# Two of the four weight sums in each block of seven products made by adding transfers instead of VectorE, in a two-layer encoder on one core

## The chip, the cores and the metric

The kernel runs on one core of one Trainium2 chip. The metric is the device time of one execution, in microseconds (us). TensorE (PE in the rows) multiplies, VectorE (DVE) and ScalarE (ACT) prepare its operands and take its results, GpSimd (POOL) and SyncE (SP) issue transfers; PEld is TensorE's weight load, which runs beside its matmuls. Each engine executes its own instructions in the order in which they are written and waits on semaphores.

## The reference, cut to what matters

Two layers, each with a mixer (differential attention, then gated linear attention) and a dense MLP, on 256 rows of 2048 values, all in float32. The change lies in the second matrix product of the two MLPs alone:

```python
def squared_relu_mlp(x, w1, w2):          # x (256, 2048), w1 (2048, 8192), w2 (8192, 2048)
    return jnp.square(jax.nn.relu(x @ w1)) @ w2
...
    for i in range(DEPTH):                # DEPTH = 2
        ...
        f = squared_relu_mlp(h, mlp_w1[i], mlp_w2[i])
        h = layer_norm(DN_ALPHA * h + f, ln_g[i, 1], ln_b[i, 1])
```

## The kernel before

**Splitting.** Every weight tile is 128 partitions x 4 rows x 512 columns of float32, 1 MB. A transfer issued by SP brings it into one of four slots `raw[:, j]`. ScalarE rounds it into `hi` (`split_hi`, `quarter_hi`), VectorE forms `lo = raw - hi` (`split_lo`, `quarter_lo`), and TensorE multiplies by `hi` and `lo` of the tile and of the activations. `hi` and `lo` also have four slots, so each tile goes through raw, hi, lo and TensorE in a pipeline. The counters are `raw_full[j]` (tile landed), `hi_ready`, `lo_ready`, `w_used` (TensorE is done with a tile). SP waits on `lo_ready` before it loads into a slot again.

**A chunk of the MLP.** `mlp(m)` has 4 chunks of 2048 hidden values. In each, four groups of four tiles (`up_pair`) make the hidden values. Then the second product follows, in two halves of the output's columns (`fast_pair`, q = 0 and q = 2; in the last chunk q = 2 is done by plain groups). So there are 7 such blocks in each MLP and 14 in the program. A block, called a unit here, consists of:

- seven products of one tile each, `product(g, p, ...)` with p = 0 to 6, a fast scheme for a 2 x 2 block product. They take quarters of the weight matrix and sums of quarters: the stationary operand is a part of the activations (`F`) or a sum of such parts (`forms`). Each product has 8 matmuls by `hi` and then 4 by `lo`;
- four plain tiles, "the rest" (r0 to r3 below), L763 to L771, 24 matmuls each.

**The quarters.** `load_quarters` brings W00, W01, W11, W10 into slots 0, 1, 2, 3. VectorE makes four sums in place with `w_sum` (L1454): slot 0 += slot 1 (for product 1), slot 1 += slot 2 (for product 4), slot 0 += slot 2 (for product 2), slot 3 += slot 0 (for product 6). Products 0, 3 and 5 take W00, W10 and W11 as loaded. Between these, VectorE adds the products' results to `res` with `add_part` (L1465); TensorE may start a product that accumulates in a bank only when `res_added` tells that the bank was read.

**Names in the text.** T0 is the start of a unit's product 0 on TensorE. "lo p" is VectorE's `quarter_lo` for product p, "hi p" ScalarE's `quarter_hi`. `first_adds` and `second_adds` add the results of the previous unit's rest tiles. `load_rest` loads r0 to r3. POOL has nothing to do while the MLPs' units run, except for a load of the layer norm's vectors at the end of each MLP.

Of the kernel before, what the change touches and what calls it, by code (L numbers as in the profile page):

```python
# [26 lines left out]
F32 = mybir.dt.float32  # L27
# [60 lines left out]
SUMMED = [0, 8 * CHUNKS - 4]  # L88
# [4 lines left out]
def build(nc, x, attn_w_qkv, attn_w_o, attn_lambda, attn_subln, gla_w_in, gla_w_gk2, gla_b_gk,  # L93
          gla_norm, gla_w_o, mlp_w1, mlp_w2, ln_g, ln_b, out):
    ctx = ExitStack()
    with ctx:
# [125 lines left out]
        w_summed = sem("w_summed")  # L222
        set_up = sem("set_up")
# [72 lines left out]
        def _(sp):  # L296
# [7 lines left out]
            def load_quarters(g, w, row, q):  # L304

                for j, (k, n) in enumerate(((0, 0), (0, 1), (1, 1), (1, 0))):
                    sp.wait_ge(lo_ready, 4 * g + j - 3)
# [30 lines left out]
            def load_mlp(m):  # L338
                for ch in range(CHUNKS):
                    with sp.Fori(0, QUARTERS) as q:  # L340
                        load_group(STEP * ch + q + G_MLP[m], w_1[m], D * ch + COLS * q)
                    load_quarters(STEP * ch + (G_MLP[m] + 4), w_2[m], KT * ch, 0)
                    load_rest(STEP * ch + (G_MLP[m] + 6), w_2[m], KT * ch, 0)
                    if ch < CHUNKS - 1:
                        load_quarters(STEP * ch + (G_MLP[m] + 7), w_2[m], KT * ch, 2)
                        load_rest(STEP * ch + (G_MLP[m] + 9), w_2[m], KT * ch, 2)
# [22 lines left out]
        def _(pool):  # L369
            def load_gb(layer, i):  # L370
                for n, src in enumerate((ln_g, ln_b)):
                    pool.dma_start(ln_gb[:, n, :], src[layer, i].partition_broadcast(P)).then_inc(gb_loaded, 16)

# [47 lines left out]
            scale_residual(1)  # L421
            pool.wait_ge(w_used, 4 * (G_MLP[0] + STEP * (CHUNKS - 1) + 6))
# [47 lines left out]
            scale_residual(3)  # L470
            pool.wait_ge(w_used, 4 * (G_MLP[1] + STEP * (CHUNKS - 1) + 6))
# [417 lines left out]
        def _(act):  # L889
            def split_hi(g, j, f=None):  # L890

                act.wait_ge(raw_full[j], 16 * (g if f is None else f) + 16)
                if not isinstance(g, int) or g:
                    act.wait_ge(w_used, 4 * g + j - 3)
                act.activation(hi[:, j], raw[:, j], ACT.Copy).then_inc(hi_ready, 1)  # L895
# [5 lines left out]
            def split_all(g, f=None):  # L901
                split_some(g, TILES, f)
# [137 lines left out]
            def quarter_hi(g, p, j, f, w):  # L1040

                if p in (0, 3, 5):
                    act.wait_ge(raw_full[j], 16 * f + 16)
                else:
                    act.wait_ge(w_summed, w + {1: 1, 2: 3, 4: 2, 6: 4}[p])
# [25 lines left out]
            def chunk(m, ch, g, f, n, first, last):  # L1071

                k = 8 * ch + 32 * m
                u = 4 * ch + FORMED[m]
                w = 8 * ch + SUMMED[m]
# [11 lines left out]
                for p, j in ((0, 0), (1, 0), (2, 0), (3, 3), (4, 1), (5, 2), (6, 3)):  # L1087
                    quarter_hi(g + 4, p, j, f + 4, w)
                down_halves(g + 3, n + 3, 1, k + 6, u + 4, False)
                split_some(g + 6, 2, f + 5)  # L1090
                f_hi_of(1, k + 6, 12)
                split_hi(g + 6, 2, f + 5)
                split_hi(g + 6, 3, f + 5)
                if last:
                    split_all(g + 7, f + 6)
                    split_all(g + 8, f + 7)
                else:
                    for p, j in ((0, 0), (1, 0), (2, 0), (3, 3), (4, 1), (5, 2), (6, 3)):
# [108 lines left out]
        def _(dve):  # L1207
            def split_lo(g, j):

                dve.wait_ge(hi_ready, 4 * g + j + 1)  # L1210
                dve.tensor_tensor(lo[:, j], raw[:, j], hi[:, j].bitcast(F32), ALU.subtract).then_inc(lo_ready, 1)  # L1211
# [290 lines left out]

            def fast_adds(s, reads, b, q):

                add_part(0, q, b, 4 * s + 1)
                quarter_lo(s, 3, 3)
                w_sum(3, 0)
                add_part(0, q + 1, b, 4 * s + 3, ALU.subtract)
                quarter_lo(s, 4, 1)
                add_part(1, q + 1, b + 1, 4 * s + 2)  # L1510
                quarter_lo(s, 5, 2)
                dve.wait_ge(res_added, reads + 3)
                add_part(1, q + 1, b, 4 * s + 5, ALU.subtract)
                quarter_lo(s, 6, 3)
# [13 lines left out]
            def chunk(m, ch, g, f, n, r, w, first, last):  # L1528
# [253 lines left out]
```

## Time and profile before

| | |
|---|---|
| median of 3 runs | 2183.89 us (2183.36 to 2185.74) |
| profiled execution, its own time | 2181.14 us |
| its span | 2179.4 us |
| PE / PEld busy | 2160.6 / 1845.6 us |
| DVE / ACT / POOL busy | 1544.2 / 995.5 / 110.3 us |
| granted TensorE clock, mean | 0.998 |
| moved by DMA | 417.20 MB, mean 191 GB/s |

The difference between an execution's time and its span is 1.7 us here and lies outside the kernel's instructions. Busy times are unions of an engine's instructions. A matmul's end is modelled and overlaps the next one, so a short wait of TensorE may not show as idle time on PE; it shows as idle time before a weight load on PEld, and as a late start.

### The profile page before, as it was taken

The numbers are of one execution on the slowest core, as the hardware profiler recorded it, in microseconds if no ns is written. First come the engines' busy times: TensorE is split into PE (matmuls) and PEld (weight loads), VectorE is DVE, ScalarE is ACT, GpSimd is POOL, SyncE is SP. The second block draws the span as 40 slices with busy tenths as digits, with TensorE's granted clock in tenths as the row PEclk, the third lists the DMA queues.
The fourth block names the chain that finished last, engine by engine and source line by source line (L and its number), as shares of the span: only waits on it lengthen the run. The fifth ranks groups of instructions, "written<-read, shape, count | busy, mean of one in ns | idle before, by whom it ended". The sixth has DMA issues, their size and how long they took to land.

```text
span 2179.4 us, 27756 instructions
## 1 busy us (share of the span) xinstructions
PE 2160.6 (99%) x11162; PEld 1845.6 (85%) x11162; DVE 1544.2 (71%) x1292; ACT 995.5 (46%) x831; POOL 110.3 (5%) x95
## 2 busy tenths in 40 slices
PE   9999999999999999999999999999999999999997
PEld 8888888988888888888888888889878888888886
DVE  5554555879678678767776566658796796786686
ACT  5443543445445444444454344334454454454541
POOL 3000000200000000000020111102000000000000
PEclk9999999999999999999999999999999999999999
DMA  9545546545754854764546445646367448547552
GB/s 318 169 156 176 181 178 220 176 134 186 264 167 154 272 190 154 250 191 183 204 140 230 160 155 185 234 158 208 103 236 245 135 168 275 173 154 270 188 209 105
DMA packets 206653, 417.20 MB, mean 191 GB/s; under 512 B 6688, under 2 KB 6688, under 8 KB 205552
## 3 DMA queue, kind: packets, MB, share of 16 engines
q1 hardware_dynamic: 204672, 406.09, 54.7%
q0 software_dynamic: 1472, 9.25, 1.2%
q8 instruction: 55, 0.90, 0.2%
q10 hardware_dynamic: 432, 0.79, 0.1%
q14 instruction: 22, 0.18, 0.0%
HBM read 414.00 MB, written 2.10 MB: 191 GB/s over the span
## 4 chain that ended last, share of the span: by engine, by line
PE 84%; DVE 7%; DMA 4%; issue 2%; ACT 2%; POOLq 0%; POOL 0%; DVEq 0%; ACTq 0%; SPq 0%
PE ps L479 71%; PE ps L719 5%; DMA raw<-in_mlp_w_dram 4%; DVE lo L1450 2%; PE ps L763 2%; PE ps L765 2%; PE ps L771 2%; DVE raw L1454 2%; ACT hi L895 1%; DVE lo L1211 1%; ACT hi L1047 1%; PE ps L550 1%; DVE res L1465 1%; DMA res<-in_x_dram 0%; PE ps L648 0%
## 5 line engine op out<-in xcount | busy, mean ns | idle before, releaser
L1211 DVE TENSOR_TENSOR lo<-raw,hi 128x2048 fp32r<-128x2048 f32 x328 | 751.2, 2304 | 328.6 <-ACT hi L895 326.7
L895 ACT ACTIVATE hi<-raw 128x2048 fp32r<-128x2048 f32 x327 | 624.1, 1916 | 584.9 <-PE ps L479 412.6
L479 PE MATMUL ps<-X,hi 128*128 128x512 f32 (+1 forms) x3008 | 700.1, 378 | 1.5 <-DVE X L1223 0.9
L479 PEld LDWEIGHTS ps<-X,hi 128*128 128x128 f32 x3008 | 542.7, 189 | 95.6 <-DVE X L1223 1.1
L479 PE MATMUL ps<-X,lo 128*128 128x256 f32 x2816 | 386.9, 283 | 0.0
L479 PEld LDWEIGHTS ps<-X,lo 128*128 128x128 f32 x2816 | 373.2, 191 | 12.8
L1047 ACT ACTIVATE hi<-raw 128x2048 fp32r<-128x2048 f32 x98 | 186.3, 1917 | 199.9 <-DVE raw L1454 142.9
L1450 DVE TENSOR_TENSOR lo<-raw,hi 128x2048 fp32r<-128x2048 f32 x98 | 224.1, 2287 | 33.0 <-ACT hi L1047 33.0
L479 PE MATMUL ps<-hi,X 128*128 128x512 f32 x768 | 246.7, 396 | 0.0
L479 PE MATMUL ps<-hi,F 128*128 128x512 f32 x768 | 241.0, 391 | 0.1
L763 PE MATMUL ps<-hi,F 128*128 128x512 f32 x448 | 175.0, 391 | 2.5 <-ACT hi L895 2.4
L765 PE MATMUL ps<-hi,F 128*128 128x512 f32 x448 | 174.4, 389 | 0.0
L479 PEld LDWEIGHTS ps<-hi,F 128*128 128x128 f32 x768 | 144.2, 188 | 30.8 <-DVE lo L1211 0.9
L479 PEld LDWEIGHTS ps<-hi,X 128*128 128x128 f32 x768 | 144.2, 188 | 30.6 <-issue 1.0
L479 PE MATMUL ps<-lo,X 128*128 128x512 f32 x384 | 149.6, 389 | 0.0
L479 PE MATMUL ps<-lo,F 128*128 128x512 f32 x384 | 149.5, 389 | 0.0
L1454 DVE TENSOR_TENSOR raw<-raw 128x2048 f32<-128x2048 f32 x56 | 126.8, 2285 | 0.0
L719 PE MATMUL ps<-hi,forms 128*128 128x512 f32 x448 | 111.2, 390 | 1.4 <-DVE res L1465 1.4
L771 PE MATMUL ps<-lo,F 128*128 128x512 f32 x448 | 110.6, 389 | 0.0
L763 PEld LDWEIGHTS ps<-hi,F 128*128 128x128 f32 x448 | 84.1, 188 | 22.4 <-ACT hi L895 5.1
L1465 DVE TENSOR_TENSOR res<-res,ps 128x512 f32<-128x512 f32 x112 | 74.1, 682 | 38.3 <-PE ps L719 19.2
L719 PEld LDWEIGHTS ps<-hi,forms 128*128 128x128 f32 x448 | 83.8, 188 | 20.3 <-issue 1.8
(141 smaller groups left out, 1533.1 us busy)
## 6 DMA issues: line engine op xcount, KB each, us to landing
raw<-in_mlp_w_dram SPq DMA_DIRECT2D x256, 1024.0 KB, 5.9
raw<-in_gla_w_in_dram SPq DMA_DIRECT2D x48, 1024.0 KB, 5.3
raw<-in_attn_w_qkv_dram SPq DMA_DIRECT2D x47, 1024.0 KB, 5.2
raw<-in_attn_w_o_dram SPq DMA_DIRECT2D x16, 1024.0 KB, 5.9
raw<-in_gla_w_o_dram SPq DMA_DIRECT2D x16, 1024.0 KB, 6.5
work<-in_ln_g_dram POOLq DMA_DIRECT2D x4, 1024.0 KB, 7.9
work<-in_ln_b_dram POOLq DMA_DIRECT2D x4, 1024.0 KB, 10.3
out_dram<-res SPq DMA_DIRECT2D x8, 256.0 KB, 2.5
```

The lines of the kernel that those rows point to most:

```text
L479: return pe.matmul(o, w, m, start=start, stop=stop)
L550: m = pe.transpose(ps[:, LN_BANKS[i % 3], blk(b)], res[:, t, blk(4 * q + b)], ident[:, :])
L719: return pe.matmul(o, w, m, start=first, stop=last or not start, skip_group_check=not start)
L763: pe.matmul(acc, F[:, a, 0, blk(t)], hi[:, p, k, :], start=first, stop=True, skip_group_check=not first)
L765: pe.matmul(acc, F[:, a, 1, blk(t)], hi[:, p, k, :], start=False, stop=True, skip_group_check=True)
L771: e = pe.matmul(acc, F[:, 4 * j + k, 0, blk(t)], lo[:, p, k, :], start=False, stop=True, skip_group_check=True)
L895: act.activation(hi[:, j], raw[:, j], ACT.Copy).then_inc(hi_ready, 1)
L1047: act.activation(hi[:, p % TILES], raw[:, j], ACT.Copy).then_inc(hi_ready, 2 if p == PRODUCTS - 1 else 1)
L1211: dve.tensor_tensor(lo[:, j], raw[:, j], hi[:, j].bitcast(F32), ALU.subtract).then_inc(lo_ready, 1)
L1450: dve.tensor_tensor(lo[:, p % TILES], raw[:, j], hi[:, p % TILES].bitcast(F32), ALU.subtract).then_inc(lo_ready, 2 if p == PRODUCTS - 1 el ...
L1454: dve.tensor_tensor(raw[:, j], raw[:, j], raw[:, k], ALU.add).then_inc(w_summed, 1)
L1465: dve.tensor_tensor(d, d, ps[:, bank, :], op).then_inc(res_added, 1)
```

## The change

Two of the four sums leave VectorE. `weight_sums` on POOL issues a transfer from DRAM with `accum_op=ADD`, which adds a weight quarter to what is in the slot: W11 onto slot b (W01) once VectorE has used W01 in its first sum, and W10 onto slot a (W00+W01+W11) once lo 2 is done. The other two sums stay on VectorE. Product 4 now waits for `third_added` and product 6 for `fourth_added`. The number of SP's loads is the same; POOL issues 28 more transfers of 1 MB.

Slots have roles a, b, c, d instead of fixed numbers. Slot d (W10) is no longer summed into, so it is free after lo 3, b after lo 4, c after lo 5 and a, the last, after lo 6. `load_rest` fills them in that order (d, b, c, a), where it before filled slot 0 and 1 after lo 4. The next unit's roles turn accordingly (`SLOTS`, `TURNED`). In the last chunk the roles are set so that the plain groups behind find slots 0 to 3 in order.

On VectorE lo 2 moves behind the first `add_part`, and `first_adds` no longer stands between sums. On ScalarE the hi of r0 moves ahead of `down_halves`.

```diff
+SLOTS = (0, 1, 2, 3)
+TURNED = (3, 1, 2, 0)
...
-            def load_rest(g, w, row, q):
-
-                for j, (n, k) in enumerate(((0, 2), (1, 2), (0, 3), (1, 3))):
-                    sp.wait_ge(lo_ready, 4 * g - (3, 3, 2, 0)[j])
+            def load_rest(g, w, row, q, slots):
+
+                for i, (j, (n, k)) in enumerate(zip(slots, ((0, 2), (1, 2), (0, 3), (1, 3)))):
+                    sp.wait_ge(lo_ready, 4 * g - (4, 3, 2, 0)[i])
...
+            def weight_sums(m):
+
+                for u in range(UNITS[1]):
+                    ch, q = u // 2, u % 2 * 2
+                    a, b = (SLOTS if ch < CHUNKS - 1 and q == 0 else TURNED)[:2]
+                    below = w_2[m][:, KT * ch + KPT:KT * ch + 2 * KPT, :]
+                    pool.wait_ge(w_summed, 2 * (UNITS[m] + u) + 1)
+                    pool.dma_start(raw[:, b], below[:, :, (q + 1) * COLS:(q + 2) * COLS], accum_op=ALU.add
+                                   ).then_inc(third_added, 16)
+                    pool.wait_ge(lo_ready, 4 * (G_MLP[m] + STEP * ch + (4 if q == 0 else 7)) + 3)
+                    pool.dma_start(raw[:, a], below[:, :, q * COLS:(q + 1) * COLS], accum_op=ALU.add
+                                   ).then_inc(fourth_added, 16)
...
+            def quarters_hi(g, f, u, slots):
+
+                a, b, c, d = slots
+                quarter_hi(g, 0, a, raw_full[a], 16 * f + 16)
+                quarter_hi(g, 1, a, w_summed, 2 * u + 1)
+                quarter_hi(g, 2, a, w_summed, 2 * u + 2)
+                quarter_hi(g, 3, d, raw_full[d], 16 * f + 16)
+                quarter_hi(g, 4, b, third_added, 16 * u + 16)
+                quarter_hi(g, 5, c, raw_full[c], 16 * f + 16)
+                quarter_hi(g, 6, a, fourth_added, 16 * u + 16)
...
-            def quarter_sums(s, f, between=None):
-
-                quarter_lo(s, 0, 0)
-                dve.wait_ge(raw_full[1], 16 * f + 16)
-                w_sum(0, 1)
-                dve.wait_ge(raw_full[2], 16 * f + 16)
-                w_sum(1, 2)
-                quarter_lo(s, 1, 0)
-                w_sum(0, 2)
-                if between:
-                    between()
-                quarter_lo(s, 2, 0)
-
-            def fast_adds(s, reads, b, q):
-
+            def quarter_sums(s, f, slots):
+
+                a, b, c, _ = slots
+                quarter_lo(s, 0, a)
+                dve.wait_ge(raw_full[b], 16 * f + 16)
+                w_sum(a, b)
+                quarter_lo(s, 1, a)
+                dve.wait_ge(raw_full[c], 16 * f + 16)
+                w_sum(a, c)
+
+            def fast_adds(s, reads, b, q, slots):
+
+                w, x, y, z = slots
                 add_part(0, q, b, 4 * s + 1)
-                quarter_lo(s, 3, 3)
-                w_sum(3, 0)
+                quarter_lo(s, 2, w)
+                quarter_lo(s, 3, z)
                 add_part(0, q + 1, b, 4 * s + 3, ALU.subtract)
-                quarter_lo(s, 4, 1)
                 add_part(1, q + 1, b + 1, 4 * s + 2)
-                quarter_lo(s, 5, 2)
+                quarter_lo(s, 4, x)
+                quarter_lo(s, 5, y)
                 dve.wait_ge(res_added, reads + 3)
                 add_part(1, q + 1, b, 4 * s + 5, ALU.subtract)
-                quarter_lo(s, 6, 3)
+                quarter_lo(s, 6, w)
...
                 if not last:
-                    quarter_sums(g + 7, f + 6, lambda: first_adds(g + 4, 2 * r, 0, 0))
-                    fast_adds(g + 7, 2 * r + 6, 4, 2)
+                    quarter_sums(g + 7, f + 6, TURNED)
+                    first_adds(g + 4, 2 * r, 0, 0)
+                    fast_adds(g + 7, 2 * r + 6, 4, 2, TURNED)
```

VectorE in the unit q = 2 of a chunk, before: lo 0 (L1450), two sums (L1454), lo 1, a sum, the two `first_adds` (L1465), lo 2, then `add_part`, lo 3 and the fourth sum, and so on to lo 6.

```order
L1450 TENSOR_TENSOR lo<-raw,hi 128x2048
L1454 TENSOR_TENSOR raw<-raw 128x2048 x2
L1450 TENSOR_TENSOR lo<-raw,hi 128x2048
L1454 TENSOR_TENSOR raw<-raw 128x2048
L1465 TENSOR_TENSOR res<-res,ps 128x512 x2
L1450 TENSOR_TENSOR lo<-raw,hi 128x2048
L1465 TENSOR_TENSOR res<-res,ps 128x512
L1450 TENSOR_TENSOR lo<-raw,hi 128x2048
L1454 TENSOR_TENSOR raw<-raw 128x2048
L1465 TENSOR_TENSOR res<-res,ps 128x512
L1450 TENSOR_TENSOR lo<-raw,hi 128x2048
```

The same stretch of the changed kernel (L1481 is `quarter_lo`, L1485 `w_sum`, L1496 `add_part`), from lo 0 to lo 6:

```order
L1481 TENSOR_TENSOR lo<-raw,hi 128x2048
L1485 TENSOR_TENSOR raw<-raw 128x2048
L1481 TENSOR_TENSOR lo<-raw,hi 128x2048
L1485 TENSOR_TENSOR raw<-raw 128x2048
L1496 TENSOR_TENSOR res<-res,ps 128x512 x3
L1481 TENSOR_TENSOR lo<-raw,hi 128x2048 x2
L1496 TENSOR_TENSOR res<-res,ps 128x512 x2
L1481 TENSOR_TENSOR lo<-raw,hi 128x2048 x2
L1496 TENSOR_TENSOR res<-res,ps 128x512
L1481 TENSOR_TENSOR lo<-raw,hi 128x2048
```

Two sums are gone, the two `first_adds` and the unit's first `add_part` now stand in one row before lo 2, and lo 2 and lo 3 follow one another.

ScalarE of the changed kernel at the end of the first unit's products in a chunk, with the semaphores (L1066 is `quarter_hi`, the last L916 are the rest tiles, L1092 `down_halves`):

```order
L1066 ACTIVATE hi<-raw 128x2048 [waits w_used,raw_full0]
L1066 ACTIVATE hi<-raw 128x2048 [waits w_used,w_summed] x2
L1066 ACTIVATE hi<-raw 128x2048 [waits w_used,raw_full3]
L1066 ACTIVATE hi<-raw 128x2048 [waits w_used,third_added]
L1066 ACTIVATE hi<-raw 128x2048 [waits w_used,raw_full2]
L1066 ACTIVATE hi<-raw 128x2048 [waits w_used,fourth_added]
L916 ACTIVATE hi<-raw 128x2048 [waits w_used,raw_full3]
L1092 ACTIVATE work<-ps 128x512 [waits form_summed,f_lo,w_used]
L1092 ACTIVATE work<-ps 128x512
L916 ACTIVATE hi<-raw 128x2048 [waits w_used,raw_full1]
```

hi 4 and hi 6 waited for VectorE's `w_summed` before; now they wait for the two adding transfers, and the hi of r0, `down_halves` and all later tiles stand behind hi 6.

## Rows read from the trace of the kernel before

**Rows 1.** The page, part 1: busy us, share, instructions.

```profile
PE 2160.6 (99%) x11162; PEld 1845.6 (85%) x11162; DVE 1544.2 (71%) x1292; ACT 995.5 (46%) x831; POOL 110.3 (5%) x95
```

**Rows 2.** Groups by line and shape: busy us, mean ns | idle before, releasers.

```profile
L1450 DVE TENSOR_TENSOR lo<-raw,hi 128x2048 fp32r<-128x2048 f32 x98 | 224.1, 2287 | 33.0 <-ACT hi L1047 33.0
L1047 ACT ACTIVATE hi<-raw 128x2048 fp32r<-128x2048 f32 x98 | 186.3, 1917 | 199.9 <-DVE raw L1454 142.9 <-PE ps L479 26.8 <-PE ps L719 19.5
L479 PEld LDWEIGHTS ps<-hi,F 128*128 128x128 f32 x768 | 144.2, 188 | 30.8 <-DVE lo L1211 0.9
L1454 DVE TENSOR_TENSOR raw<-raw 128x2048 f32<-128x2048 f32 x56 | 126.8, 2285 | 0.0
L763 PEld LDWEIGHTS ps<-hi,F 128*128 128x128 f32 x448 | 84.1, 188 | 22.4 <-ACT hi L895 5.1
L719 PEld LDWEIGHTS ps<-hi,forms 128*128 128x128 f32 x448 | 83.8, 188 | 20.3 <-issue 1.8 <-DVE res L1465 1.2
L1465 DVE TENSOR_TENSOR res<-res,ps 128x512 f32<-128x512 f32 x112 | 74.1, 682 | 38.3 <-PE ps L719 19.2 <-PE ps L771 19.1
L719 PEld LDWEIGHTS ps<-lo,F 128*128 128x128 f32 x168 | 31.3, 188 | 6.9 <-DVE lo L1450 0.5
```

**Rows 3.** PEld in order of time: start, us, what [idle before <- releaser].

```profile
703.69 1.68 PEld L719 LDWEIGHTS ps<-hi,forms 128*128 128x128 f32 x8 [0.87 <-issue]
...
1629.38 0.19 PEld L763 LDWEIGHTS ps<-hi,F 128*128 128x128 f32 x1 [1.97 <-ACT hi L895]
```

**Rows 4.** PE in order of time, a unit q = 2 of the first MLP.

```profile
700.37 1.98 PE L719 MATMUL ps<-hi,forms 128*128 128x512 f32 x8
702.18 1.07 PE L719 MATMUL ps<-lo,forms 128*128 128x512 f32 x4
703.70 2.10 PE L719 MATMUL ps<-hi,forms 128*128 128x512 f32 x8 [0.45 <-DVE res L1465]
```

**Rows 5.** The chain that ended last: start, us, what.

```profile
567.94 89.04 PE ps L479 x512
...
710.80 5.08 DMA raw<-in_mlp_w_dram
...
740.02 89.04 PE ps L479 x512
...
911.05 89.04 PE ps L479 x512
...
1621.03 6.36 DMA raw<-in_mlp_w_dram
```

**Rows 6.** DVE in order of time, the same unit q = 2.

```profile
687.51 2.29 DVE L1450 TENSOR_TENSOR lo<-raw,hi 128x2048 fp32r<-128x2048 f32 x1 [0.86 <-ACT hi L1047]
...
700.68 2.29 DVE L1450 TENSOR_TENSOR lo<-raw,hi 128x2048 fp32r<-128x2048 f32 x1 [0.87 <-ACT hi L1047]
702.89 0.68 DVE L1465 TENSOR_TENSOR res<-res,ps 128x512 f32<-128x512 f32 x1
703.48 2.29 DVE L1450 TENSOR_TENSOR lo<-raw,hi 128x2048 fp32r<-128x2048 f32 x1
```

**Rows 7.** A lone 1 MB load issued by POOL: its issue row, and us to landing.

```profile
318.69 0.61 POOL L372 DMA_DIRECT2D work<-in_ln_g_dram  x1 [4.85 <-PE ps L648]
...
work<-in_ln_g_dram POOLq DMA_DIRECT2D x1, 1024.0 KB, 4.7
```

**Rows 8.** The transfers in 1015 to 1045: GB/s in 40 slices, and issues.

```profile
GB/s 404 404 388 388 396 380 388 385 393 388 390 456 418 396 404 391 415 423 418 355 407 380 388 390 382 385 393 388 382 388 385 388 300 363 407 390 229 287 399 369
...
work<-in_ln_g_dram POOLq DMA_DIRECT2D x1, 1024.0 KB, 9.1
work<-in_ln_b_dram POOLq DMA_DIRECT2D x1, 1024.0 KB, 11.7
```

**Rows 9.** Busy us by stage: PE, PEld, DVE, ACT, POOL, PEclk, DMA share, GB/s.

```profile
672.00:698.00 26.00, 26.00 (x116) 21.52 (x115) 24.69 (x16) 12.65 (x8) 0.00 (x0) 1.00 0.80 291
698.00:740.00 42.00, 41.24 (x181) 33.43 (x180) 35.45 (x24) 22.69 (x12) 0.00 (x0) 1.00 0.65 228
```

More of the change, by code:

```diff
@@ L87 @@
 FORMED = [0, 4 * CHUNKS]
-SUMMED = [0, 8 * CHUNKS - 4]
+SLOTS = (0, 1, 2, 3)
+TURNED = (3, 1, 2, 0)
 UNITS = [0, 2 * CHUNKS - 1]
@@ L222, in build @@
         w_summed = sem("w_summed")
+        third_added = sem("third_added")
+        fourth_added = sem("fourth_added")
         set_up = sem("set_up")
@@ L302, in load_group, with load_quarters @@
                                  ).then_inc(raw_full[j], 16)
-            def load_quarters(g, w, row, q):
-                for j, (k, n) in enumerate(((0, 0), (0, 1), (1, 1), (1, 0))):
-                    sp.wait_ge(lo_ready, 4 * g + j - 3)
+            def load_quarters(g, w, row, q, slots, quarters=((0, 0), (0, 1), (1, 1), (1, 0))):
+                for i, (j, (k, n)) in enumerate(zip(slots, quarters)):
+                    sp.wait_ge(lo_ready, 4 * g + i - 3)
                     sp.dma_start(raw[:, j], w[:, bass.ds(row + KPT * k, KPT), (q + n) * COLS:(q + n + 1) * COLS]
                                  ).then_inc(raw_full[j], 16)
-            def load_rest(g, w, row, q):
-                for j, (n, k) in enumerate(((0, 2), (1, 2), (0, 3), (1, 3))):
-                    sp.wait_ge(lo_ready, 4 * g - (3, 3, 2, 0)[j])
+            def load_rest(g, w, row, q, slots):
+                for i, (j, (n, k)) in enumerate(zip(slots, ((0, 2), (1, 2), (0, 3), (1, 3)))):
+                    sp.wait_ge(lo_ready, 4 * g - (4, 3, 2, 0)[i])
                     sp.dma_start(raw[:, j], w[:, bass.ds(row + KPT * k, KPT), (q + n) * COLS:(q + n + 1) * COLS]
@@ L421, in _ @@
             scale_residual(1)
+            weight_sums(0)
             pool.wait_ge(w_used, 4 * (G_MLP[0] + STEP * (CHUNKS - 1) + 6))
@@ L470, in _ @@
             scale_residual(3)
+            weight_sums(1)
             pool.wait_ge(w_used, 4 * (G_MLP[1] + STEP * (CHUNKS - 1) + 6))
@@ L889, in _, with split_hi @@
         def _(act):
-            def split_hi(g, j, f=None):
-                act.wait_ge(raw_full[j], 16 * (g if f is None else f) + 16)
+            def split_hi(g, j, f=None, slots=SLOTS):
+                act.wait_ge(raw_full[slots[j]], 16 * (g if f is None else f) + 16)
                 if not isinstance(g, int) or g:
                     act.wait_ge(w_used, 4 * g + j - 3)
-                act.activation(hi[:, j], raw[:, j], ACT.Copy).then_inc(hi_ready, 1)
+                act.activation(hi[:, j], raw[:, slots[j]], ACT.Copy).then_inc(hi_ready, 1)
             def split_some(g, n, f=None):
@@ L899, in split_some, with split_all @@
                     split_hi(g, j, f)
-            def split_all(g, f=None):
-                split_some(g, TILES, f)
+            def split_all(g, f=None, slots=SLOTS):
+                for j in range(TILES):
+                    split_hi(g, j, f, slots)
             def copy_halves(g, n, par, dst, slots=2, scale=1.0):
@@ L1037, in _, with quarter_hi @@
             ln_window(G_WO + 3, 1)
[L1040 to L1045, printed above, removed]
+            def quarter_hi(g, p, j, ready, count):
+                act.wait_ge(ready, count)
                 act.wait_ge(w_used, 4 * g + p - 3)
@@ L1074, in chunk @@
                 u = 4 * ch + FORMED[m]
-                w = 8 * ch + SUMMED[m]
+                v = 2 * ch + UNITS[m]
+                first_slots, rest_slots = (TURNED, SLOTS) if last else (SLOTS, TURNED)
                 for e in range(3):
@@ L1086, in chunk @@
                         form_hi_of(S4, 1, u + 4)
-                for p, j in ((0, 0), (1, 0), (2, 0), (3, 3), (4, 1), (5, 2), (6, 3)):
-                    quarter_hi(g + 4, p, j, f + 4, w)
+                quarters_hi(g + 4, f + 4, v, first_slots)
+                split_hi(g + 6, 0, f + 5, rest_slots)
                 down_halves(g + 3, n + 3, 1, k + 6, u + 4, False)
-                split_some(g + 6, 2, f + 5)
+                split_hi(g + 6, 1, f + 5, rest_slots)
+                split_hi(g + 6, 2, f + 5, rest_slots)
                 f_hi_of(1, k + 6, 12)
-                split_hi(g + 6, 2, f + 5)
-                split_hi(g + 6, 3, f + 5)
+                split_hi(g + 6, 3, f + 5, rest_slots)
                 if last:
@@ L1097, in chunk @@
                 else:
-                    for p, j in ((0, 0), (1, 0), (2, 0), (3, 3), (4, 1), (5, 2), (6, 3)):
-                        quarter_hi(g + 7, p, j, f + 6, w + 4)
+                    quarters_hi(g + 7, f + 6, v + 1, TURNED)
                     split_all(g + 9, f + 7)
@@ L1207, in _, with split_lo @@
         def _(dve):
-            def split_lo(g, j):
+            def split_lo(g, j, slots=SLOTS):
                 dve.wait_ge(hi_ready, 4 * g + j + 1)
-                dve.tensor_tensor(lo[:, j], raw[:, j], hi[:, j].bitcast(F32), ALU.subtract).then_inc(lo_ready, 1)
+                dve.tensor_tensor(lo[:, j], raw[:, slots[j]], hi[:, j].bitcast(F32), ALU.subtract
+                                  ).then_inc(lo_ready, 1)
             def split_some(g, n):
```

24 lines of the change are left out of this document (14 added, 10 removed).

## The prediction

> **What bounds the kernel now.** I read the page's part 1 first. PE is busy 2160.6 us of a span of 2179.4 us, so 99% of the time is TensorE's own work, which the change leaves as it is; DVE is at 71% and POOL at 5% [rows 1]. Taking work from VectorE can therefore only give back time in which TensorE waits for it. The second reading is how much that is in the fourteen units. PE's own idle time hides short waits, so I take the weight loads, whose idle time has its releaser [rows 2]. Three groups belong to the units. L719 on `forms` waited 1.8 us for "issue" and 1.2 us for VectorE's additions to `res`; the 1.8 us are two pauses like the one at 703.69, whose matmul half is put down to DVE res in the PE row of the same moment [rows 3, 4]. L763, the first matmul of the rest tiles, waited 5.1 us for hi of r0. L719 on lo,F waited 0.5 us for lo 6. The sum is 8.6 us. The 0.9 us of L479 for lo belong to the plain group behind the last unit, which the change doesn't touch; they stay.
>
> What causes these waits is seen in order of time in one unit [rows 4, 6]. lo 2 starts at 700.68, after a queue of sums and two additions, and only behind it, at 702.89, VectorE reads the bank of product 0, ending at 703.57. TensorE began product 1 at 700.37 and was ready for product 2 2.72 us later (12 matmuls; products 0 to 6 follow at this pitch, the 8 matmuls by `hi` taking 1.81 of it, since 700.37 to 702.18 is 1.81). It should have started at 703.09 and started at 703.70: 0.61 us late. The second wait is a chain that the last view shows: slot 0 comes free when lo 4 ends, the load of r0 is issued at 710.80 and takes 5.08 us, then comes hi of r0, and TensorE is waiting for it. At 1621.03 the same load took 6.36 us, and the pause behind it was 1.97 us [rows 3, 5].
>
> **What can be gained.** A pause on PEld isn't all delay, since the weight load runs ahead. At 703.69 the pause is 0.87 us and the delay 0.61 us, so 0.26 us less. With 13 pauses (0.15 to 1.97 us) and 3 of them below 0.26 us (0.15, 0.16 and 0.20, which then cost nothing) the delays come to 8.6 - 0.5 - 10 x 0.26 = 5.5 us. From above, 8.6 us less the pause of 0.04 us that stands between any two loads (pitch 2.72 / 12 = 0.227 us, load 0.188 us), 13 times, is 8.1 us. A check from the loop's two passes: 740.02 - 567.94 = 172.08 us and 911.05 - 740.02 = 171.03 us [rows 5]. TensorE's own work in a pass is 89.04 us of hidden groups, 14 products of 2.72 us and 8 rest tiles of 24 x 0.227 = 5.44 us: 170.6 us. So 1.4 and 0.4 us are lost in these two passes, where I count delays of 1.1 and 0.2 us by the first way. The truth lies between the ends; I take **6 us** as what there is to gain.
>
> **The change part by part.**
>
> *Two sums of each unit leave VectorE:* 28 x 2.285 = 64 us of its work [rows 2]. TensorE sees of this only that the queue ahead of lo 2 is shorter. In the new order of the unit q = 2, lo 0 starts at 687.51 as before, the sum at 689.7, lo 1 when hi 1 is there at about 694.0 (the sum's end at 691.9 plus 1.92 us, and handing over), the second sum ends at 698.4, `first_adds` at 699.7, and the first `add_part` then has to wait for product 0, T0 + 2.72 = 700.37, and ends at 701.1. Product 2 (due at 703.09) no longer waits. lo 2 ends at 703.3, and the `lo` half of product 2 is due at 704.9. lo 3, 4, 5 and 6 follow with their additions at 705.5, 709.8, 712.0 and 714.9, due at 707.6, 710.3, 713.1 and 715.8. The narrowest is lo 4, by 0.5 us. So the waits of L719 (3.0 and 0.5 us of pause) go.
>
> *The slots:* the load of r0 is issued when lo 3 ends, at about 705.5 instead of 710.8. With 5.1 to 6.4 us [rows 5] it lands at 710.6 to 711.9, and hi of r0 has to start 1.92 us ahead of T0 + 19.04 = 716.7, at 714.8. There are 3 us to spare, so the 5.1 us of pause go as well, in the worst unit too (1.97 us). r1 is issued at lo 4 as before; r2 at lo 5; r3 at lo 6, also as before. In the last chunk slot a is loaded after slots b, c and d; its first hi is then due some 10 us after the load lands. These cost nothing, and what hides them is the 5.44 us that TensorE spends on each rest tile and the 5.57 us on each hidden tile (89.04 / 16).
>
> *`down_halves` and lo 2 moved back:* `down_halves` now stands behind hi of r0; what it feeds is needed by r2, 10.9 us after r0 starts. lo 2 stands behind `add_part`, in the units q = 0 too, and so ends at T0 + 2.72 + 0.68 + 2.2 = T0 + 5.7. TensorE needs it at T0 + 7.25. But the **fourth** adding transfer starts only then.
>
> *The third adding transfer* (W11) is released by the first sum's end at 691.9. hi 4 must start 1.92 + 2.29 us ahead of 710.3, at 706.1. Its window is 14 us.
>
> *The fourth* (W10) is released at T0 + 5.7. Product 6's `lo` half is due at T0 + 6 x 2.72 + 1.81 = T0 + 18.1; less lo 6 (2.29) and hi 6 (1.92), hi 6 must start at T0 + 13.9. **Its window is 8.2 us**, the same in all 14 units, and everything beyond it is a stall of TensorE: hi 6 holds up on ScalarE hi of r0 and `down_halves`, lo 6 on VectorE lo of r0, and slot a's next load. This is the term that decides.
>
> No row of this trace shows an adding transfer. The nearest is POOL's lone load of 1 MB: 4.7 us from issue to landing, of which 0.61 us is the issue [rows 7]. That is the lower end; I see no reason for an addition to be quicker. The destination must be read as well, 1 MB more through the same 16 engines; at 388 GB/s, the usual slice of a full stream [rows 8], 1.05 MB takes 2.7 us. Alone it is then 4.7 to 7.4 us. Beside it runs r0's load, issued 2.2 us later (lo 3's 2.2 us), which can take up to 2.7 us of the engines' time from it: upper end 10.1 us. That sharing is real is seen where POOL's load met SP's full stream: 9.1 us for the first, 11.7 us for the second [rows 8]. I take half of the second read (1.3 us), as reading and writing can go side by side, and half of the shared time (1.3 us), as the addition has a start: **7.3 us**, inside the window by 0.9 us. The added 29 MB are bearable as a mean: in the units the transfers' share is 0.80 and 0.65 [rows 9], and a unit of 40.8 us carries 8 MB, 22 us of engines' time; two additions at twice the price make it 32 us.
>
> **The sum:** -6 us, + 0 for the additions, + 0 for the moves. 2181.14 - 6 = 2175.1 us for an execution like the profiled one. This is 2.75 us below the median of the runs shown; by the median, 2183.89 - 6 = **2178 us**.
>
> *A rule that speaks against it.* Row first: a lone load of POOL's takes 4.7 us [rows 7], and how much the second read adds no row shows. The Trainium skill, Collectives: The Full Stack, section "Why ReduceScatter is half of AllGather", says that a summing transfer needs two source reads on the same ring and so runs at half a copy's rate. By that the fourth takes the upper end and is late in each unit; that is the first rival below, and its price is worked out there from rows.
>
> **The rivals.** A measurement of this kernel can tell about 0.2%, 4.4 us.
>
> 1. *The fourth addition is late* (slower). Mechanism: it is paid at twice a copy, and r0's load comes in between. Price at the upper end: 10.1 - 8.2 = 1.9 us in 14 units, 27 us, less the 6 us: 2183.9 + 21 = 2205 us. It decides from a delay of 6 / 14 = 0.43 us a unit, that is from 8.6 us to landing; above 8.9 us the kernel is measurably slower. For it: the margin is only 0.9 us and rests on two halves that I chose. Against it: engines half free at that moment (0.65). Chance 0.27 (late by 0.7 to 3 us).
> 2. *A summing transfer is much slower*, at a quarter of a copy's rate: 4.7 + 3 x 2.7 = 12.8 us, the fourth late by 4.6 us, 14 x 4.6 = 64 us: 2242 us; with r0's load beside it, the third comes near its 14 us too. No row excludes it. Chance 0.10.
> 3. *It lands about at the window's end* (8.4 to 8.9 us): what is won is given back, 2180 to 2188 us. Chance 0.15.
> 4. *The waits stay*: r0's load comes 5 us earlier but shares with the addition, and VectorE's queue was late for other reasons; or only the 3.5 us of L719's pauses go. 2181 to 2184 us. Chance 0.06.
> 5. *The forecast*: both additions fit, the waits go, 2175.5 to 2179.5 us. Chance 0.42.
>
> **How the numbers follow.** The likeliest is case 5, 2178 us. Its own range is 2175.5 (8.1 us gained) to 2179.5. Since cases of both signs hold the chance, the full range is wider: it starts at 2175 and reaches up into rival 1. Above 2213 I leave rival 2 (0.10) and the last part of rival 1 (0.07). Faster by over 0.2% (below 2179.5): case 5, less a little for a gain nearer 4 us: 0.40. Within 0.2%: rival 3, rival 4 and that little: 0.23. Slower: rivals 1 and 2: 0.37.
>
> **What would show it.** Right: the idle time of L763's weight load before hi of r0 falls from 5.1 us to under 0.5, that of L719 on `forms` from 3.0 us to none; L1454's count halves to 28; 28 additions of POOL's land in under 8.2 us (the fourth) and 14 us (the third); hi 6 waits for the previous product on PE, as hi 5 does. Wrong: an idle time before the last product's weight loads in each unit, released by hi 6 or lo 6, with ScalarE's wait for the transfer ahead of it; then the step that failed is the price of the second read or of the sharing. If the fourth is in time and the gain is still absent, it is the step from pauses to delays. The narrowest on VectorE is lo 4, by 0.5 us: an idle time before product 4's `lo` would show that my timeline is off.

## The result and the profile after

The changed kernel takes **2201.79 us** (median of 5 runs, 2201.44 to 2203.95), the kernel before 2183.85 us in the same job (2182.49 to 2185.74): 1.0085 times, 95% interval 1.007 to 1.010. It is slower by 18 us; 2178 us were forecast, and the first rival gave 2205 us. The profiled execution's span is 2199.4 us, against 2179.4 us.

The changed kernel's page, part 1, as in [rows 1]:

```profile
PE 2165.7 (98%) x11162; PEld 1845.2 (84%) x11162; DVE 1482.9 (67%) x1264; ACT 991.4 (45%) x831; POOL 146.1 (7%) x123
```

VectorE did lose 28 instructions and 61 us of busy time, and TensorE executes the same 11162 matmuls. The groups by line and shape, with idle time and releasers, for the lines of [rows 2] (L740 is `product`, L784 the rest tiles, L500 the plain groups, L1485 `w_sum`):

```profile
L500 PEld LDWEIGHTS ps<-hi,F 128*128 128x128 f32 x768 | 144.2, 188 | 29.9
L784 PEld LDWEIGHTS ps<-hi,F 128*128 128x128 f32 x448 | 84.1, 188 | 17.7
L740 PEld LDWEIGHTS ps<-hi,forms 128*128 128x128 f32 x448 | 84.1, 188 | 17.4
L1485 DVE TENSOR_TENSOR raw<-raw 128x2048 f32<-128x2048 f32 x28 | 64.0, 2285 | 0.0
L740 PEld LDWEIGHTS ps<-hi,F 128*128 128x128 f32 x336 | 61.5, 188 | 33.2 <-ACT hi L1066 11.7 <-issue 9.5
L740 PEld LDWEIGHTS ps<-lo,F 128*128 128x128 f32 x168 | 30.4, 188 | 15.2 <-DVE lo L1481 9.6
```

The reader sees both halves of the result here. All pauses of before are gone: the 5.1 us before the rest tiles, the 3.0 us on `forms`, and the 0.9 us of the plain group, too, which I had left standing. New are 21.2 us before product 6's `hi` matmuls (11.7 put down to ACT hi and 9.5 to "issue", all at this one place) and 9.6 us before its `lo` matmuls. In order of time, TensorE at the end of the products of a unit q = 0 (T0 = 660.51):

```profile
674.14 1.98 PE L740 MATMUL ps<-hi,forms 128*128 128x512 f32 x8
675.96 1.07 PE L740 MATMUL ps<-lo,forms 128*128 128x512 f32 x4
677.97 2.11 PE L740 MATMUL ps<-hi,F 128*128 128x512 f32 x8 [0.95 <-ACT hi L1066]
680.37 1.21 PE L740 MATMUL ps<-lo,F 128*128 128x512 f32 x4 [0.28 <-DVE lo L1481]
```

Product 6 was due at 674.14 + 2.72 = 676.86 and starts 1.11 us late; its `lo` matmuls, 1.81 us later in the products before, come 2.40 us later. What they waited for, from POOL, ScalarE and VectorE in order of time:

```profile
650.75 1.27 POOL L387 DMA_DIRECT2D raw<-in_mlp_w_dram  x1 [114.40 <-DVE raw L1485]
666.65 1.27 POOL L390 DMA_DIRECT2D raw<-in_mlp_w_dram  x1 [14.62 <-DVE lo L1481]
...
676.01 1.91 ACT L1066 ACTIVATE hi<-raw 128x2048 fp32r<-128x2048 f32 x1 [7.90 <-DMA raw<-in_mlp_w_dram]
...
678.02 2.29 DVE L1481 TENSOR_TENSOR lo<-raw,hi 128x2048 fp32r<-128x2048 f32 x1 [2.83 <-ACT hi L1066]
```

The fourth addition is issued at T0 + 6.1 and lands some 9.3 us later, and hi 6 and lo 6 follow at once. All 14 units have these two pauses: from 571.64 to 746.03 in the chain, a pass of the loop takes 174.39 us, where TensorE's own work is 170.6 us (e3 below measures it as 170.67), so 1.9 us are lost in each of its two units. The additions by line, with us to landing (min/median/max), L387 the third and L390 the fourth:

```profile
L387 POOL DMA_DIRECT2D raw<-in_mlp_w_dram x14: 1273/1282/1368, 476.0 to 2097.0; - x14
...
DMA to landing us min/median/max: 8.3/8.4/9.5
...
L390 POOL DMA_DIRECT2D raw<-in_mlp_w_dram x14: 1274/1283/1301, 491.9 to 2108.1; - x14
...
DMA to landing us min/median/max: 9.1/9.3/9.8
```

The third's landing at the fastest, 8.3 us, is that of an addition alone: in the stretch around the one at 650.75 no other queue moved a byte.

### The profile page after: what moved, and what is told of

Read it like the earlier page. It is cut to its first block, busy times and chain, and to the rows that moved or that the text cites. A ratio compares the mean times of both kernels' runs of the same rounds, so it can differ in the third digit from the quotient of the medians.

```text
span 2199.4 us, 27776 instructions
## 1 busy us (share of the span) xinstructions
PE 2165.7 (98%) x11162; PEld 1845.2 (84%) x11162; DVE 1482.9 (67%) x1264; ACT 991.4 (45%) x831; POOL 146.1 (7%) x123
## 4 chain that ended last, share of the span: by engine, by line
PE 88%; DMA 6%; DVE 3%; ACT 1%; issue 1%; POOLq 0%; POOL 0%; DVEq 0%; ACTq 0%
PE ps L500 70%; DMA raw<-in_mlp_w_dram 6%; PE ps L784 5%; PE ps L786 5%; PE ps L792 5%; DVE lo L1481 3%; PE ps L740 3%; ACT hi L1066 1%; PE ps L571 1%; DVE res L1496 0%; DMA res<-in_x_dram 0%; PE ps L669 0%; PE ps L881 0%; DVE res L1435 0%; PE ps L650 0%
## 5 line engine op out<-in xcount | busy, mean ns | idle before, releaser
L916 ACT ACTIVATE hi<-raw 128x2048 fp32r<-128x2048 f32 x327 | 623.8, 1915 | 511.6 <-PE ps L500 412.8
L500 PE MATMUL ps<-X,hi 128*128 128x512 f32 (+1 forms) x3008 | 700.0, 378 | 1.4 <-DVE X L1254 0.8
L500 PEld LDWEIGHTS ps<-X,hi 128*128 128x128 f32 x3008 | 542.6, 189 | 95.6 <-DVE X L1254 1.0
L500 PE MATMUL ps<-X,lo 128*128 128x256 f32 x2816 | 386.9, 283 | 0.0
L500 PEld LDWEIGHTS ps<-X,lo 128*128 128x128 f32 x2816 | 373.1, 191 | 12.8
L1066 ACT ACTIVATE hi<-raw 128x2048 fp32r<-128x2048 f32 x98 | 185.1, 1912 | 287.2 <-DVE raw L1485 135.4
L1481 DVE TENSOR_TENSOR lo<-raw,hi 128x2048 fp32r<-128x2048 f32 x98 | 221.9, 2288 | 87.3 <-ACT hi L1066 87.3
L500 PE MATMUL ps<-hi,X 128*128 128x512 f32 x768 | 246.7, 396 | 0.0
L500 PE MATMUL ps<-hi,F 128*128 128x512 f32 x768 | 240.5, 391 | 0.0
L784 PE MATMUL ps<-hi,F 128*128 128x512 f32 x448 | 174.4, 389 | 0.0
L786 PE MATMUL ps<-hi,F 128*128 128x512 f32 x448 | 174.4, 389 | 0.0
L500 PEld LDWEIGHTS ps<-hi,X 128*128 128x128 f32 x768 | 144.2, 188 | 30.7 <-issue 1.0
L500 PEld LDWEIGHTS ps<-hi,F 128*128 128x128 f32 x768 | 144.2, 188 | 29.9
L500 PE MATMUL ps<-lo,X 128*128 128x512 f32 x384 | 149.6, 389 | 0.0
L500 PE MATMUL ps<-lo,F 128*128 128x512 f32 x384 | 149.5, 389 | 0.0
L1496 DVE TENSOR_TENSOR res<-res,ps 128x512 f32<-128x512 f32 x112 | 73.0, 683 | 77.4 <-PE ps L740 54.5
L740 PE MATMUL ps<-hi,forms 128*128 128x512 f32 x448 | 110.6, 389 | 0.0
L740 PE MATMUL ps<-hi,F 128*128 128x512 f32 x336 | 85.0, 395 | 15.5 <-ACT hi L1066 15.5
L784 PEld LDWEIGHTS ps<-hi,F 128*128 128x128 f32 x448 | 84.1, 188 | 17.7
L786 PEld LDWEIGHTS ps<-hi,F 128*128 128x128 f32 x448 | 84.1, 188 | 17.7
```

What stands on the lines that cost most here:

```text
L500: return pe.matmul(o, w, m, start=start, stop=stop)
L740: return pe.matmul(o, w, m, start=first, stop=last or not start, skip_group_check=not start)
L784: pe.matmul(acc, F[:, a, 0, blk(t)], hi[:, p, k, :], start=first, stop=True, skip_group_check=not first)
L786: pe.matmul(acc, F[:, a, 1, blk(t)], hi[:, p, k, :], start=False, stop=True, skip_group_check=True)
L916: act.activation(hi[:, j], raw[:, slots[j]], ACT.Copy).then_inc(hi_ready, 1)
L1066: act.activation(hi[:, p % TILES], raw[:, j], ACT.Copy).then_inc(hi_ready, 2 if p == PRODUCTS - 1 else 1)
```

## The experiments

All times are beside runs of the kernel before on the same chip. The first job: 2184.06 us before (21 runs).

**e1_plain** takes the addition out of POOL's transfers.

```diff
-                    pool.dma_start(raw[:, b], below[...], accum_op=ALU.add
+                    pool.dma_start(raw[:, b], below[...]
...
-                    pool.dma_start(raw[:, a], below[...], accum_op=ALU.add
+                    pool.dma_start(raw[:, a], below[...]
```

> The changed kernel with POOL's 28 transfers as plain copies of the same bytes into the same slots, not additions; the products therefore take other weights, and only the time is read. Theory (the addition itself is dear: in the changed kernel a lone one takes 8.3 us to landing, and moves data at 213 GB/s where loads move 388): a plain copy lands in 5 to 6 us, the fourth fits its window of 8.2 us, the pause before product 6 goes, and the time is near 2176 us. Rival (POOL's issue of 512 rows of 2 KB is what is slow, not the addition): the issue stays at 1.28 us and the landing above 8 us, 2195 to 2202 us.

Measured: 2174.23 us (4 runs), 0.9956 times (0.9941 to 0.9971). The fourth's rows in it:

```profile
L390 POOL DMA_DIRECT2D raw<-in_mlp_w_dram x14: 748/748/758, 492.0 to 2082.8; - x14
...
DMA to landing us min/median/max: 5.3/5.5/6.3
```

The theory holds: the same bytes, issued behind the same waits, leave no pause of TensorE's in the units when they aren't added. The issue is 0.75 us instead of 1.28 us, and the data move twice as fast. What the transfers moved, in slices of 0.3 us around the third addition of the changed kernel (650 to 662), and of 0.25 us around the plain copy in its place (646 to 656). The full slices of the first (those between the first and the last 218) have a mean of 208 GB/s (my expectation has 213), those of the second (393 to 393) of 411 GB/s:

```profile
GB/s 0 0 0 0 0 0 0 0 0 116 61 82 130 143 218 212 198 218 198 218 212 212 191 198 212 218 191 218 48 0 0 0 0 0 0 0 0 0 0 0
```

```profile
GB/s 0 0 0 0 0 0 0 0 131 66 33 147 393 377 410 442 442 410 410 426 393 115 0 0 0 0 0 0 0 0 0 0 0 0 0 0 0 0 0 0
```

**e2_r0_late** keeps the additions and moves r0's load back to where it was.

```diff
-                    sp.wait_ge(lo_ready, 4 * g - (4, 3, 2, 0)[i])
+                    sp.wait_ge(lo_ready, 4 * g - (3, 3, 2, 0)[i])
```

> The changed kernel with r0's load released by lo 4, as before the change, instead of lo 3, so that nothing shares the DMA engines with the fourth addition at first. Theory (most of the fourth's 9.2 us is its own, sharing adds 0.9 us): it lands in 8.3 to 8.5 us, each unit loses about 1.0 us instead of 1.9, and 14 x 0.9 = 12 us are gained: about 2190 us, less if r0 now comes late again. Rival (the fourth is slow for its place, for VectorE or POOL, not for sharing): it stays at 9.2 us and the time at 2202 us.

Measured: 2189.47 us (10 runs), 1.0027 times (1.0018 to 1.0036); the fourth lands in 8.2/8.4/8.7 us, like the third. So 12.3 us of the time, 0.9 us a unit, is the sharing with r0's load. The other 15.3 us (2189.47 - 2174.19, with e3 below), 1.1 us a unit, TensorE loses by the addition's own 8.4 us.

**e3_no_fourth** leaves the fourth addition out.

```diff
-                    pool.wait_ge(lo_ready, 4 * (G_MLP[m] + STEP * ch + (4 if q == 0 else 7)) + 3)
-                    pool.dma_start(raw[:, a], below[...], accum_op=ALU.add).then_inc(fourth_added, 16)
...
-                quarter_hi(g, 6, a, fourth_added, 16 * u + 16)
+                quarter_hi(g, 6, a, w_summed, 2 * u + 2)
```

> The changed kernel without the fourth addition: product 6 takes slot a without W10, and only the time is read. It shows what the rest of the change gives. By the delays counted in the trace of before, 5.5 us (2178 us); by the pauses, 8.1 us (2176 us). Rival (something else in the change costs, too, such as the third addition or the order on ScalarE): 2182 us or more.

Measured: 2174.19 us (5 runs), 0.9955 times (0.9941 to 0.9968). Its chain, at the start of three passes of the loop:

```profile
567.07 89.04 PE ps L497 x512
...
737.74 89.04 PE ps L497 x512
...
908.41 89.04 PE ps L497 x512
```

A pass takes 170.67 us, which is TensorE's own work to 0.1 us, and no weight load in the units has a pause before it. The rest of the change gives 9.9 us, and the fourth addition costs 2201.8 - 2174.2 = 27.6 us, 1.97 us a unit. The third costs nothing that can be seen.

**e4_lo2_early** and **e5_lo2_ahead** let the fourth addition start earlier. In both, lo 2 stands at the end of `quarter_sums` instead of behind the first `add_part`. e4 has `first_adds` between the first sum and lo 1, e5 has it behind the second sum.

```diff
                 w_sum(a, b)
+                if between:                  # e4: here
+                    between()
                 quarter_lo(s, 1, a)
                 w_sum(a, c)
+                if between:                  # e5: here instead
+                    between()
+                quarter_lo(s, 2, a)
...
                 add_part(0, q, b, 4 * s + 1)
-                quarter_lo(s, 2, w)
                 quarter_lo(s, 3, z)
```

> The changed kernel with lo 2 put back behind the second sum, ahead of the first add_part, and first_adds between the first sum and lo 1, so that the fourth addition starts earlier: in the units q = 0 by 4 to 5 us, in the units q = 2 by 2 to 3 us. Same transfers, same sums. Theory (the fourth is late only because of when it is released): the windows become over 10 us against 9.2, the pause before product 6 goes in all units, about 2176 us. Rival (the additions harm by what they move, or the new order makes product 2 wait for add_part, as before the change): some of it stays, 2180 to 2190 us.

Measured: 2181.86 us (11 runs), 0.9992 times (0.9983 to 1.0001). VectorE in a unit q = 2 of e4, at `first_adds` and at lo 2:

```profile
692.27 1.28 DVE L1496 TENSOR_TENSOR res<-res,ps 128x512 f32<-128x512 f32 x2 [1.90 <-PE ps L792]
...
700.03 2.29 DVE L1481 TENSOR_TENSOR lo<-raw,hi 128x2048 fp32r<-128x2048 f32 x1 [2.06 <-ACT hi L1066]
```

In the first three chunks of each MLP the units q = 0 had no pause any more. There the fourth addition is issued at T0 + 1.1 instead of T0 + 6.1. The units q = 2 had one of 0.5 to 0.7 us before product 6's `lo`: `first_adds` waits for r2's matmuls, lo 1, the second sum and lo 2 wait behind it, and the addition is issued at T0 + 5.1. The second half of the rival came as well: product 2 waited for `add_part`, with pauses of 0.3 us in each unit q = 2 and of 1.1 and 0.9 us in the two last chunks, where product 6's `lo` still waited 0.6 to 0.7 us. So the theory is right for six of the 14 units, and my new order had waits of its own in the others. e5 was made to see whether that is all.

> The changed kernel with lo 2 ahead of the first add_part, as in the run e4_lo2_early, but with first_adds behind the second sum, while ScalarE makes hi 2. In e4 first_adds waited 1.9 us for r2 in front of lo 1 and so cost the units q = 2 some 1.6 us. Theory (only the release of the fourth addition counts): its window is over 10 us in both kinds of unit against 9.2 us, and the time falls from 2182 us to about 2175 us, but for the last chunk's units, where slot a is loaded last and the first add_part would come late (1.1 us each). Rival (additions disturb in other ways too): it stays near 2182 us.

Measured (second job, before 2183.12 us, 22 runs): 2176.93 us (7 runs), 0.9971 times (0.9959 to 0.9982). With all 28 additions in place the kernel is faster than before. Against the changed kernel only the place of lo 2 differs, and so the fourth's start: it is issued at T0 + 1.1 in the units q = 0, at T0 + 3.9 to 4.6 in the units q = 2 and at T0 + 5.8 in the last chunks, where it was T0 + 6.1 in all. The fourth addition's issue in the unit q = 0 with T0 = 656.23:

```profile
657.38 1.27 POOL L390 DMA_DIRECT2D raw<-in_mlp_w_dram  x1 [9.63 <-DVE lo L1481]
```

Left are pauses of 0.2 to 0.4 us in two units and, as expected, 1.0 and 0.6 us in each last chunk.

**e6_fourth_dve** puts the fourth sum back on VectorE, in the slots' new order (e5's order otherwise); r0's load waits for that sum.

```diff
                 quarter_lo(s, 3, z)
+                w_sum(w, z)
...
+                    if i == 0:
+                        sp.wait_ge(w_summed, 3 * summed + 3)
```

> e5_lo2_ahead with the fourth sum on VectorE again (slot a += slot d behind lo 3) and only the third as an adding transfer; r0's load is released by that sum, 2.2 us later than by lo 3. Theory (VectorE needs relief in the units q = 2 only, and one sum of 2.3 us gives enough; no window of 8 us is left): no pauses, 2174 to 2176 us. Rival (the fourth sum between lo 3 and lo 4 makes lo 4 or an add_part late again, by up to 0.9 us in six units, or r0 comes late): 2178 to 2181 us.

Measured: 2176.77 us (7 runs), 0.9968 times (0.9957 to 0.9980). The time is e5's, a little above what I expected. TensorE waits for no transfer in the units, but VectorE is late by 0.2 us in one of them and in each last chunk, with pauses of 1.0 to 1.1 us before product 2 and of 0.7 us before product 4's `lo`.

**e7_slots_alone** takes the third addition away as well; the rest of its order is e6's.

```diff
                 w_sum(a, b)
+                dve.wait_ge(raw_full[c], 16 * f + 16)
+                w_sum(b, c)
                 quarter_lo(s, 1, a)
-                dve.wait_ge(raw_full[c], 16 * f + 16)
                 w_sum(a, c)
```

> No adding transfers at all: all four sums on VectorE (slot b += slot c before lo 1, slot a += slot d behind lo 3), but the slots' roles and the order of the rest's loads as in the change, r0's load released by the fourth sum. It shows what the slots' order is worth by itself. By the pauses of before, L763's 5.1 us go, less the run-ahead of the loads: 3.5 to 5 us, and with lo 2 ahead of add_part the 3.0 us of L719 stay or grow: 2179 to 2181 us. Rival (the slots' order is worth nothing without the relief): 2184 us.

Measured: 2176.73 us (8 runs), 0.9972 times (0.9961 to 0.9982). **Neither branch of what I expected came: it gives as much as e6**, though VectorE does all the work of before. From the start of the first unit to that of the last it takes 512.0 us in each MLP, as e3 does, three passes of TensorE's own work; left are the pauses of the last chunks (1.17 and 0.68 us, 1.01 and 0.67 us). Two rows of it in a unit q = 2, lo 0 and lo 2 (T0 = 696.59):

```profile
684.97 2.28 DVE L1479 TENSOR_TENSOR lo<-raw,hi 128x2048 fp32r<-128x2048 f32 x1
...
698.12 2.29 DVE L1479 TENSOR_TENSOR lo<-raw,hi 128x2048 fp32r<-128x2048 f32 x1 [0.87 <-ACT hi L1064]
```

lo 0 starts 11.6 us ahead of T0, where it was 10.1 us in [rows 6] (T0 = 697.64), and lo 2 starts 1.5 us after T0 instead of 3.0. The first quarter of this unit is loaded once VectorE is done with r0 of the unit q = 0 ahead of it. That `lo`, VectorE's `add_halves` (L1472 before, L1501 here) and SP's loads of the quarters, before (T0 = 656.82) and in e7 (T0 = 655.76):

```profile
673.61 1.28 DVE L1472 TENSOR_TENSOR work<-ps,work 128x512 f32<-128x512 f32 x2
675.34 2.29 DVE L1211 TENSOR_TENSOR lo<-raw,hi 128x2048 fp32r<-128x2048 f32 x1 [0.45 <-ACT hi L895]
...
677.66 9.38 SPq L308 DMA_DIRECT2D raw<-in_mlp_w_dram  x4
```

```profile
672.55 2.28 DVE L1239 TENSOR_TENSOR lo<-raw,hi 128x2048 fp32r<-128x2048 f32 x1
674.76 1.28 DVE L1501 TENSOR_TENSOR work<-ps,work 128x512 f32<-128x512 f32 x2
...
674.86 10.58 SPq L311 DMA_DIRECT2D raw<-in_mlp_w_dram  x4
```

The quarters' loads start at T0 + 19.1 instead of T0 + 20.8. **Two parts of the change work together here, and only one of them is the slots' order.** The slots' order has r0 loaded earlier. The other part is missing in the list of moves under "The change": in the units q = 0, VectorE's `lo` of r0, r1 and r2 moved ahead of `add_halves`, `square` and `f_lo_of`, and ScalarE's `hi` of r2 ahead of `f_hi_of`. e7 keeps these moves. By the rows, an estimate: with `add_halves` still ahead of it the `lo` of r0 would start 1.2 us later, so that the slots' order alone would bring 0.5 of the 1.7 us; the move alone would bring nothing, since the `lo` of before waits for hi of r0. No run has one without the other. In the unit q = 2 itself SP starts to load the rest tiles at T0 + 8.9 (705.44) instead of T0 + 13.2 (710.80); about 1 us of that is VectorE's earlier start, the rest is the slots' order.

**e8_third_alone** is the counterpart: the kernel before with its second sum as an addition of POOL's.

```diff
                 w_sum(0, 1)
                 dve.wait_ge(raw_full[2], 16 * f + 16)
-                w_sum(1, 2)
                 quarter_lo(s, 1, 0)
                 w_sum(0, 2)
```

> The kernel before with one edit: its second sum (slot 1 += slot 2) is an adding transfer of POOL's, slots and orders as before. It shows what relief of VectorE by one sum is worth by itself. The addition takes 8.3 us and has some 14 us. By the pauses of before, L719's 3.0 and 0.5 us go and L763's 5.1 us stay: 2181 to 2182 us. Rival (the addition shares with the loads and makes r0 or the quarters later): 2184 us or more.

Measured: 2182.34 us (11 runs), 0.9998 times (0.9989 to 1.0007): no difference. VectorE in the unit q = 2, lo 1 and lo 2 (T0 = 698.18):

```profile
694.50 2.29 DVE L1464 TENSOR_TENSOR lo<-raw,hi 128x2048 fp32r<-128x2048 f32 x1 [2.06 <-ACT hi L1060]
...
701.06 2.29 DVE L1464 TENSOR_TENSOR lo<-raw,hi 128x2048 fp32r<-128x2048 f32 x1 [0.87 <-ACT hi L1060]
```

Where the sum stood, VectorE is now idle for 2.06 us, since lo 1 needs hi 1, and hi 1 needs the first sum. lo 2 starts 2.9 us after T0, against 3.0. The fourth sum, which stands in no such gap but ahead of lo 4, was not taken away in the old order by itself.

**e9_last_order**, last, is e7 with two moves on VectorE.

```diff
+                if late:                     # in the last chunk: lo 2 behind the first add_part
+                    quarter_lo(s, 2, w)
...
-                add_part(1, q + 1, b + 1, 4 * s + 2)
                 quarter_lo(s, 4, x)
+                add_part(1, q + 1, b + 1, 4 * s + 2)
```

> e7_slots_alone (no adding transfers, the slots' order of the change) with two moves on VectorE: in the last chunk's unit the first add_part stands ahead of lo 2, since slot a is loaded last there, and in all units the third add_part stands behind lo 4 as before the change. The only pauses left in e7 are 1.17 and 0.68 us, and 1.01 and 0.67 us, in the two last chunks. Theory (nothing else of TensorE's waits is left in the units): about 2 us less, 2174 to 2175.5 us, as without the fourth addition. Rival (lo 4 or lo 5 falls due instead): 2176.5 us.

Measured (third job, before 2183.31 us, 9 runs): 2175.25 us (5 runs), 0.9961 times (0.9947 to 0.9974). It has the lowest time of the kernels that compute the whole reference, with no adding transfer in it, though its interval overlaps those of e5, e6 and e7. Small pauses are left in each last chunk, 0.2 us before product 4 and 0.5, 0.2 and 0.2 us before the `lo` matmuls of products 4, 5 and 6, so a little of the rival came too.

## Why the prediction was wrong, by its own steps

**The step that failed is the price of an adding transfer.** I put it at 4.7 to 7.4 us alone and took 7.3 us with r0's load beside it, against a window of 8.2 us. It takes 8.3 to 8.4 us alone and 9.3 us beside r0's load. By terms:

- *The start:* I took the plain load's 4.7 us as it stood. A plain copy of this shape (512 rows of 2 KB) takes 5.3 us, 0.75 us of it issue (e1), and the addition's issue takes 1.28 us.
- *The second read:* I took half of 2.7 us. Alone, the addition takes 8.3 - 5.3 = 3.0 us more than the copy, 0.5 us of it issue. The data move at 208 GB/s in place of 411 GB/s. I had halved the term on the thought that reading and writing go side by side; the runs show nothing of that saving. The full 2.7 us, my upper end, would have been near for this term; my upper end for the whole, 7.4 us, still lay below the measured 8.3 us, so it was no bound.
- *The sharing:* I took 1.3 us, measured are 0.9 us (e2).
- *The release:* I had T0 + 5.7; POOL's issue begins at T0 + 6.1, some 0.3 us after VectorE's end.

**The window was right in kind and too long.** Everything beyond it is a stall, but it is 7.3 us from the issue to the landing and not 8.2 us. Two runs give the same: 9.3 us cost 1.97 us a unit (e3), 8.4 us cost 1.1 us a unit (e2 against e3). By the rows, 0.4 us of the difference is the late release and 0.3 us the handing over from the landing to hi 6, lo 6 and TensorE (676.01, 678.02, 680.37), for which my sum had nothing. So an addition with nothing beside it is too late as well.

Rival 1 named the place and the mechanism. Its size, 1.9 us in each of 14 units (measured 1.9 by the loop's passes, 1.97 by e3), is right partly by luck: its 10.1 us and its 8.2 us are both about 0.9 us too large, and the difference stands. I gave this rival 0.27 and the forecast 0.42.

The rule that I cited against the change, that a summing transfer runs at half a copy's rate (the Trainium skill, Collectives: The Full Stack, "Why ReduceScatter is half of AllGather"), agrees with this trace in the rate of the data, 208 GB/s against 411 GB/s. From issue to landing the addition takes 8.3 us against 5.3 us, which is less than double.

**The gain was too small in the sum:** 6 us, where e3 shows 9.9 us from median to median (an interval of 7 to 13 us). The 6 us were read from one execution of 2181.14 us, 2.9 us quicker than the median of before in e3's job. The fair comparison is with e3's profiled execution, 2173.59 us: 7.6 us less. From the first unit's start to the last one's, before takes 514.68 us in the first MLP and 516.49 us in the second, e3 512.00 us in both; that is 7.2 us for the pauses of 8.6 us. So a pause costs all but about 0.1 us, and not all but 0.26 us as in my lower way (5.5 us). The small pause before the plain group, 0.9 us, which I had left standing, went too. The other 2.3 us of the 9.9 us are how much further the profiled execution of before lies below its median than e3's does below its own; no trace shows where the other runs lose them.

**The reason for the gain was half wrong.** That r0's load comes earlier and its 5.1 us go was right. But I put the late lo 2 down to the sums queued before it, and that failed: taking one sum away alone changes nothing (e8), since it stood in a gap in which lo 1 waits for ScalarE anyway, and putting both sums back costs nothing (e6 and e7 against e5, 2176.8, 2176.7 and 2176.9 us). The queue was late because the unit's first quarter landed late; my timeline kept lo 0 at 687.51 "as before". The slots' order and the moves on VectorE together bring it 1.5 us forward (e7). So the gain comes from the new order of slots and instructions, and in that order the additions bring only their cost: e7 has no wait left but in the last chunks, and e9, with two moves more, gains 8.1 us without any addition, which the intervals don't tell from e3's 9.9 us. That the additions relieve VectorE of 64 us is true, and nothing that a run could measure came of it.

**The third addition** was right: 8.4 us (9.5 us at most) in a window of 14 us, no pause. **lo 4** with its 0.5 us to spare didn't become a pause in the changed kernel.

What stays open is how much of the gain the slots' order gives without the moves on VectorE and ScalarE that came with it, and what the fourth sum's removal alone would do in the old order. No run separates these.

## What to carry to other kernels

When a step leaves an engine for a transfer, two times have to be compared. One is the transfer's whole time from its release to its landing, with the addition and with what shares the DMA engines then. The other is the time until its reader is due, less every handing over. A mean share of 0.65 on the DMA engines says nothing about that. Before an engine is relieved, look whether the work taken away stands in front of a wait for another engine: then an idle gap takes its place. And free first the buffer whose load is waited for first: the new order of the four slots, with the instructions moved to fit it, adds no work and gave, as far as the runs can tell, all that this change had to give.

## What the runs showed of the hardware

An adding transfer of 1 MB from DRAM onto SBUF takes 8.3 us alone, against 5.3 us for a plain one of the same shape from the same queue, and moves 208 GB/s against 411. It has 528 packets where the plain one has 272, for the same 1.05 MB, and takes its engines twice as long: the software queue's share of them is 9.1% in the changed kernel, 5.1% with plain copies in place of the additions (e1) and 1.2% in the kernel before. So 29.4 MB take 7.9% when they are added and 3.9% when they are not, 0.27% for a MB against 0.13%. Beside a plain load of 1 MB that starts 2 us later an addition loses 0.9 us. VectorE's instructions (2285 and 2288 ns, before 2285 and 2287) took no longer beside them.
